# Fillers in the waits for the norms, VectorE alone for the merge sum, small matmuls padded to 128 rows

## What is computed

```
hn    = rmsnorm(h) ;  u = hn @ w_in              # q, k, v, gates of four mixers, and 4 x 1024 merge logits
y_sb, y_gla, y_ml, y_ret = four causal mixers of u, each 256 wide
merged = sum over n of sigmoid(logits_n + b_n) * (y_n @ w_branch_n)
h     = h + rmsnorm(merged @ w_out)
f     = rmsnorm(h)
h     = h + rmsnorm((silu(f @ w_gate) * (f @ w_up)) @ w_down)
```

## Time and profile before

| | |
|---|---|
| median of 3 runs | 1014.35 us (1011.94 to 1016.44) |
| profiled execution | 1014.39 us, its span 1012.6 us |
| TensorE busy | 982.7 us (97%), 7664 matmuls |
| VectorE, ScalarE, GpSimd busy | 592.2, 520.7, 128.1 us |
| mean granted clock | 0.991 |

### The profile page before, as it was taken

How to read it: one execution, slowest core, us unless ns; L and a number is a source line. 1 busy time by engine, 2 the same in 40 slices (tenths; PEclk the granted TensorE clock), 3 DMA queues, 4 the chain that set the end, 5 groups by cost and what they waited for, 6 DMA issues and landing times.

```text
span 1012.6 us, 19561 instructions
## 1 busy us (share of the span) xinstructions
PE 982.7 (97%) x7664; PEld 931.5 (92%) x7664; DVE 592.2 (58%) x870; ACT 520.7 (51%) x826; POOL 128.1 (13%) x106
## 2 busy tenths in 40 slices
PE   7999999999998999999989999999999899999997
PEld 5999888789997999999969998888999899999996
DVE  6556565346966655553465565744579656666443
ACT  4553754366466544454455437544754755454452
POOL 1000000002540222110000000000034212222010
PEclk9999999999999999999989999999999999999998
DMA  5874434246552655555545544344465536555551
GB/s 157 271 229 130 128 120 126 84 125 160 174 169 82 206 167 166 170 191 162 163 125 164 169 139 125 112 126 126 125 162 172 167 125 187 186 183 190 188 187 42
DMA packets 168523, 156.42 MB, mean 154 GB/s; under 512 B 9091, under 2 KB 167022, under 8 KB 168078
## 3 DMA queue, kind: packets, MB, share of 16 engines
q1 hardware_dynamic: 167598, 152.13, 48.7%
q10 hardware_dynamic: 672, 3.37, 1.0%
q0 software_dynamic: 192, 0.07, 0.0%
HBM read 154.50 MB, written 1.05 MB: 154 GB/s over the span
## 4 chain that ended last, share of the span: by engine, by line
PE 92%; DVE 4%; ACT 2%; issue 1%; DMA 1%; SPq 0%; DVEq 0%; ACTq 0%
PE banks L622 26%; PE banks L624 25%; PE banks L623 25%; PE banks L672 2%; PE banks L657 1%; PE banks L653 1%; PE banks L654 1%; PE banks L868 1%; DVE lo L1377 1%; PE banks L870 1%; ACT hi L1039 1%; PE banks L897 1%; PE banks L905 1%; DVE term L1648 1%; DMA xt<-in_x 1%
## 5 line engine op out<-in xcount | busy, mean ns | idle before, releaser
L622 PE MATMUL banks<-xh,hi 128*128 128x272 f32 (+1 forms) x1584 | 460.1, 290 | 2.4 <-DVE lo L1377 1.3
L1377 DVE TENSOR_TENSOR lo<-raw,hi 128x1024 fp32r<-128x1024 f32 (+1 forms) x290 | 356.4, 1232 | 174.8 <-ACT hi L1039 173.6
L624 PE MATMUL banks<-xh,lo 128*128 128x272 f32 (+1 forms) x1584 | 452.9, 286 | 0.0
L623 PE MATMUL banks<-xl,hi 128*128 128x272 f32 (+1 forms) x1584 | 452.8, 286 | 0.0
L1039 ACT ACTIVATE hi<-raw 128x1024 fp32r<-128x1024 f32 (+1 forms) x290 | 302.0, 1042 | 96.5 <-PE banks L624 58.0
L622 PEld LDWEIGHTS banks<-xh,hi 128*128 128x128 f32 x1584 | 298.5, 188 | 9.5 <-issue 6.6
L623 PEld LDWEIGHTS banks<-xl,hi 128*128 128x128 f32 x1584 | 298.0, 188 | 0.6
L624 PEld LDWEIGHTS banks<-xh,lo 128*128 128x128 f32 x1584 | 298.5, 188 | 0.0
L624 PE MATMUL banks<-ah,lo 128*128 128x272 f32 (+1 forms) x352 | 100.4, 285 | 0.0
L622 PE MATMUL banks<-ah,hi 128*128 128x272 f32 (+1 forms) x352 | 100.1, 284 | 0.0
L623 PE MATMUL banks<-al,hi 128*128 128x272 f32 (+1 forms) x352 | 99.9, 284 | 0.0
(11 more groups left out here) (252 smaller groups left out, 1176.4 us busy)
## 6 DMA issues: line engine op xcount, KB each, us to landing
raw<-in_w_in SPq DMA_DIRECT2D x54, 1024.0 KB, 5.2
raw<-in_ffn_w_gate SPq DMA_DIRECT2D x22, 1024.0 KB, 5.3
raw<-in_ffn_w_up SPq DMA_DIRECT2D x22, 1024.0 KB, 5.3
raw<-in_ffn_w_down SPq DMA_DIRECT2D x16, 1024.0 KB, 5.1
raw<-in_w_out SPq DMA_DIRECT2D x8, 1024.0 KB, 5.2
raw<-in_w_in SPq DMA_DIRECT2D x12, 512.0 KB, 4.4
raw<-in_w_branch SPq DMA_DIRECT2D x12, 512.0 KB, 5.6
raw<-in_ffn_w_down SPq DMA_DIRECT2D x8, 768.0 KB, 4.3
```

The source lines that it names most:

```text
L622: mm(dst, wh, mh, start=start, stop=False)
L623: mm(dst, wh, ml, start=False, stop=False)
L624: return mm(dst, wl, mh, start=False, stop=stop)
L1377: tt(lo[g % 2][:, 0:k, f], raw[g % 2][:, 0:k, f], hi[g % 2][:, 0:k, f].bitcast(F32), ALU.subtract).then_inc(lo_ready, 2 if g in G_MIX else 1)
```

## The change

- Fillers: eight instead of four at the start; four after `mean_square_first`, three after the mean square of layer 1's first norm, and four after the mean square of norms 1 and 3 in both layers.
- Sums of squares at the start by half rows of x, each as soon as its half has come; the first mean square is then five matmuls instead of three.
- Roundings: `round_half(0)` and its `lo` go ahead of the first root; in `gate_up` one half is rounded ahead of `root(l, 2)`, and its `lo` goes between the two gate tiles on VectorE. `add_sublayer` adds tile 0 before it scales tile 1.
- Merge: GpSimd's `merge` is gone; VectorE does both additions for every m, right behind the two products. `rest_of_merged(m)` is now in round m itself for m = 0 to 5, behind `rest_of_half`; for m = 6 and 7 in round 7. ScalarE's order is as it was.
- Padding to 128 rows: `wgate`, `gl` and `gr_rows` get 128 partitions; the meta tokens' values of heads 2 and 3 get tiles of their own (`v0b`, `v0c`), zero elsewhere, so that L868 multiplies with all rows of `pt0`. This adds memsets on VectorE (`wgate`, `v0b`, and `v0c` behind the last step of `conv`); the DMA of `wgate` on GpSimd's queue waits for its memset, and the two bias DMAs behind it too.

Not shown in the diff: the tiles' new places, two semaphores that fall away, `turn` writing through `meta_values` and waiting for five pads, and the memset of `v0b`.

```
@@ -227,7 +227,7 @@
 REST_AHEAD = 3
-WARM_START = 4
+WARM_START, WARM_FIRST, WARM_NORM, WARM_PRE = 8, 4, 4, 3
@@ -333,12 +333,12 @@
 ifbias = sb("ifbias", [P, DEPTH])
-wgate = sb("wgate", [16, DEPTH, P])
+wgate = sb("wgate", [P, DEPTH, P])
...
 ones = sb("ones", [P, T])
-gl = sb("gl", [36, T])
-gr_rows = sb("gr_rows", [36, HEADS, T])
+gl = sb("gl", [P, T])
+gr_rows = sb("gr_rows", [P, HEADS, T])
@@ -411,6 +410,12 @@
+
+def meta_values(mix, pair):
+
+    if pair == 0:
+        return M["v0"][:, mix, :]
+    return M["v0b" if mix in (SB, RET) else "v0c"][:, mix // 3 if mix in (SB, RET) else mix - GLA, :]
@@ -689,9 +694,11 @@
         ps = open_tile(t)
-        pe.wait_ge(ss_ready, 6)
-        for b, (at, n) in enumerate(((0, META), (KB1, P), (KB2, P))):
-            last = mm(ps[:, at:at + n], cut["mean"][0:n, :], sq[0:n, b, 0:n], start=True, stop=True)
+        pe.wait_ge(ss_ready, 10)
+        mm(ps[:, 0:META], cut["mean"][0:META, :], sq[0:META, 0, 0:META], start=True, stop=True)
+        for b, at in enumerate((KB1, KB2)):
+            for n in range(2):
+                last = mm(ps[:, at:at + P], cut["mean"], sq[:, 1 + 2 * b + n, 0:P], start=n == 0, stop=n == 1)
@@ -731,7 +738,7 @@
         pe.wait_ge(bias_loaded, 48)
-        close_tile(mm(open_tile(t)[:, 0:T], wgate[:, l, :], M["small"][0:16, :], start=True, stop=True), t)
+        close_tile(mm(open_tile(t)[:, 0:T], wgate[:, l, :], M["small"][:], start=True, stop=True), t)
@@ -864,8 +871,7 @@
             wait_p(l, mix, h)
-        both = head_rows[pair % 2]
-        mm(ops[:, 0:T], M["v0"][both, mix, :], M["pt0"][both, :], start=True, stop=False)
+        mm(ops[:, 0:T], meta_values(mix, pair), M["pt0"][:], start=True, stop=False)
@@ -992,14 +998,19 @@
             mean_square(l, 0, 0)
+            keep_warm(WARM_PRE)
...
             mean_square_first()
+            keep_warm(WARM_FIRST)
...
         mean_square(l, 1, q_start(l))
+        keep_warm(WARM_NORM)
...
         mean_square(l, 3, q_start(l))
+        wait_taken(pe, TILE[l]["gu"] + 2)
+        keep_warm(WARM_NORM)
@@ -1050,17 +1061,18 @@
-        ss, spare = sq[:, KT - 1, 0:3], (sub[:, 0:4, 0:256], sub[:, 4:8, 0:256])
+        ss, spare = sq[:, KT - 1, 0:5], sub[:].rearrange("p k t -> p (k t)")
         act.wait_ge(meta_loaded, 16)
-        fn(spare[0][0:META], xt[0:META, 0, :].rearrange("p (a c) -> p a c", a=4), ACT.Square, accum_out=ss[0:META, 0:1]).then_inc(ss_ready, 1)
-        act.wait_ge(x_loaded[0], 16)
-        act.wait_ge(x_loaded[1], 16)
-        for b in range(1, 3):
-            act.wait_ge(ss_ready, b)
-            fn(spare[b % 2], xt[:, b, :].rearrange("p (a c) -> p a c", a=4), ACT.Square, accum_out=ss[:, b:b + 1]).then_inc(ss_ready, 1)
-        for b, n in enumerate((META, P, P)):
-            act.wait_ge(ss_ready, 3)
-            fn(sq[0:n, b, 0:n], cut["ident"][0:n, 0:n], ACT.Copy, scale=ss[0:n, b:b + 1]).then_inc(ss_ready, 1)
+        fn(spare[0:META, 0:D], xt[0:META, 0, :], ACT.Square, accum_out=ss[0:META, 0:1]).then_inc(ss_ready, 1)
+        for n in range(2):
+            act.wait_ge(x_loaded[n], 16)
+            for b in range(1, 3):
+                at = 2 * b - 1 + n
+                act.wait_ge(ss_ready, 1)
+                fn(spare[:, 512 * (at - 1):512 * at], xt[:, b, 512 * n:512 * n + 512], ACT.Square, accum_out=ss[:, at:at + 1]).then_inc(ss_ready, 1)
+        for at, n in enumerate((META, P, P, P, P)):
+            act.wait_ge(ss_ready, 5)
+            fn(sq[0:n, at, 0:n], cut["ident"][0:n, 0:n], ACT.Copy, scale=ss[0:n, at:at + 1]).then_inc(ss_ready, 1)
@@ -1301,7 +1313,8 @@
         for c in range(2):
-            round_half(n + c)
+            if c:
+                round_half(n + 1)
@@ -1333,8 +1346,8 @@
             square_first()
+            round_half(0)
             root(l, 0, 0)
-            round_half(0)
@@ -1348,6 +1361,7 @@
         round_ffn_x(l, q0)
+        round_half(2 * G_GU[l] + ROUND_AHEAD)
@@ -1381,12 +1395,12 @@
+        if l == 0:
+            rest_of_half(0)
...
                 stt(sq[:, k, :], hT[:, k, :], par[:, l, R_MIXPRE + k:R_MIXPRE + k + 1], rstd[:], ALU.mult, ALU.mult).then_inc(xn_ready[l], 1)
-            if l == 0 and k == 1:
-                rest_of_half(0)
@@ -1400,12 +1414,19 @@
+
+        def scale(k):
+            tt(sub[:, k, q0:], sub[:, k, q0:], rstd[:, q0:], ALU.mult).then_inc(post_scaled[l], 1)
+
+        scale(0)
         for k in range(KT + 2):
+            if 0 < k < KT - 1:
+                scale(k + 1)
             if k < KT:
-                tt(sub[:, k, q0:], sub[:, k, q0:], rstd[:, q0:], ALU.mult).then_inc(post_scaled[l], 1)
-            if 0 < k <= KT:
-                dve.wait_ge(post_scaled[l], n // 2 * KT + k)
-                tt(hT[:, k - 1, q0:], hT[:, k - 1, q0:], sub[:, k - 1, q0:], ALU.add).then_inc(h_ready[l], 1)
+                dve.wait_ge(post_scaled[l], n // 2 * KT + k + 1)
+                tt(hT[:, k, q0:], hT[:, k, q0:], sub[:, k, q0:], ALU.add).then_inc(h_ready[l], 1)
+            if k == 0:
+                scale(1)
@@ -1477,6 +1499,9 @@
                 stt(M["mqk"][:, t, :], src, tap, M["mqk"][:, t, :], ALU.mult, ALU.add).then_inc(conv_step[l], 1)
+        if j == 3:
+            dve.wait_ge(conv_step[l], 16)
+            nc.vector.memset(M["v0c"][:], 0.0).then_inc(pad_set[l], 1)
@@ -1642,25 +1667,24 @@
             dve.wait_ge(merge_step[l], m - 1)
+        t = term[:, m % 2, :, q0:]
...
             n = slice(2 * pair, 2 * pair + 2)
-            tt(term[:, m % 2, n, q0:], branch_banks[(2 * m + pair) % 3][:, :, 0:T - q0], by_branch[:, n, m, q0:], ALU.mult).then_inc(branch_free[l], 1)
+            tt(t[:, n, :], branch_banks[(2 * m + pair) % 3][:, :, 0:T - q0], by_branch[:, n, m, q0:], ALU.mult).then_inc(branch_free[l], 1)
         if m == KT - 1:
-            last = term[:, m % 2, :, q0:]
-            dve.wait_ge(branch_free[l], 2 * KT)
-            tt(last[:, 0:2, :], last[:, 0:2, :], last[:, 2:4, :], ALU.add).then_inc(half_late[l], 1)
-            rest_of_merged(l, m - 2)
-            dve.wait_ge(half_late[l], 1)
-            dve.wait_ge(ml_ready[l], KT - 2)
-            tt(acc[:, m % 2, q0:], last[:, 0, :], last[:, 1, :], ALU.add).then_inc(half_late[l], 1)
-        else:
-            rest_of_half(at + REST_AHEAD)
-        if m and m != KT - 2:
             rest_of_merged(l, m - 1)
+        dve.wait_ge(branch_free[l], 2 * m + 2)
+        tt(t[:, 0:2, :], t[:, 0:2, :], t[:, 2:4, :], ALU.add).then_inc(half_ready[l], 1)
+        dve.wait_ge(half_ready[l], m + 1)
+        if m >= 2:
+            dve.wait_ge(ml_ready[l], m - 1)
+        tt(acc[:, m % 2, q0:], t[:, 0, :], t[:, 1, :], ALU.add).then_inc(merge_step[l], 1)
...
             rest_of_merged(l, m)
-            rest_of_half(at + REST_AHEAD)
+        rest_of_half(at + REST_AHEAD)
+        if m < KT - 2:
+            rest_of_merged(l, m)
@@ -1692,10 +1716,9 @@
-        for c in range(2):
-            gate_tile(c, t + c)
-            if c:
-                rest_of_half(n + 1)
+        gate_tile(0, t)
+        rest_of_half(n + 1)
+        gate_tile(1, t + 1)
@@ -1716,10 +1739,11 @@
     nc.vector.memset(ones[:], 1.0).then_inc(misc_set, 1)
+    nc.vector.memset(wgate[:], 0.0).then_inc(misc_set, 1)
...
     nc.vector.memset(gr_rows[:], 0.0).then_inc(misc_set, 1)
-    dve.wait_ge(misc_set, 5)
+    dve.wait_ge(misc_set, 6)
@@ -1770,27 +1794,13 @@
-    def merge(l):
-
-        q0 = q_start(l)
-        for m in range(KT - 1):
-            pool.wait_ge(branch_free[l], 2 * m + 2)
-            if m:
-                pool.wait_ge(merge_step[l], m)
-            tt(half[:, :, q0:], term[:, m % 2, 0:2, q0:], term[:, m % 2, 2:4, q0:], ALU.add).then_inc(half_ready[l], 1)
-            pool.wait_ge(half_ready[l], m + 1)
-            if m >= 2:
-                pool.wait_ge(ml_ready[l], m - 1)
-            tt(acc[:, m % 2, q0:], half[:, 0, q0:], half[:, 1, q0:], ALU.add).then_inc(merge_step[l], 1)
...
     load_rows(pool, PARAM_ROWS[7:], par_late)
-    pool.dma_start(wgate[:], gla_w_gate_up.rearrange("l r m -> r l m")).then_inc(bias_loaded, 16)
-    pool.wait_ge(misc_set, 1)
+    pool.wait_ge(misc_set, 3)
+    pool.dma_start(wgate[0:16], gla_w_gate_up.rearrange("l r m -> r l m")).then_inc(bias_loaded, 16)
...
         q0 = q_start(l)
-        merge(l)
```

More of the change, by code:

```diff
@@ L378, in build @@
                     ("conv_in", [P, 4, T + 3]), ("mqk", [P, 4, T]), ("gq", [P, T]), ("gk", [P, T]),
-                    ("gr", [P, 2, T]), ("mo", [P, 2, T]), ("rg", [P, 2, T]), ("v", [P, 2, 4, 256]), ("v0", [P, 4, P]),
+                    ("gr", [P, 2, T]), ("mo", [P, 2, T]), ("rg", [P, 2, T]), ("v", [P, 2, 4, 256]), ("v0", [P, 4, P]), ("v0b", [P, 2, P]),
                     ("pt", [P, HEADS, SCW]), ("pt0", [P, T]), ("sa", [P, 2, SCW]), ("sb2", [P, 2, SCW]),
@@ L382, in build @@
                     ("rows", [P, 3, T]), ("osb", [P, 8, T])]
-        gla_spec = [("qa", [P, SEQ]), ("qb", [P, P]), ("q0", [P, META]), ("kr0", [P, KB2]), ("kr1", [P, SEQ]), ("k00", [P, 32])]
```

(15 more changed lines are left out.)

## The result

The changed kernel takes 1023.64 us (median of 4 runs, 1022.43 to 1025.22), the kernel before 1014.28 in the same job: a ratio of 1.0094, 95% interval 1.0066 to 1.0121. It is slower by 9.4 us; predicted were 1015.5 us and a range of 1006 to 1021. The profiled execution took 1025.22 us, its span is 1023.4 against 1012.6.

What follows compares the result with a forecast made beforehand. TensorE, busy 97% of the span, was taken to bound the kernel. Gains of 15.3 us against 16.6 lost in the merge: 1014.4 - 15.3 + 16.6 = 1015.7, stated as 1015.5, range 1006 to 1021 (0.8).

Steps and rivals of the forecast that it cites:

- the ring: Merge: `lo`, transfer, `hi`, rounding of the merged tile, its rest, next `lo`: 7.5 to 8.3 us a round against TensorE's 6.07.
- Merge: Both layers' merges: 7.2 us lost in layer 0, 8.4 in layer 1, 1 for the clock of both: 16.6 (12 to 19).
- Adding tile 0 first brings the first add one scaling earlier: `add_sublayer`: 0.25 us gained at each of the three borders that TensorE waits at, 0.7 in all.
- Together 4.2: Fillers: 1.0 us back from the matmuls from 518.15, 3.2 from two half-clock stretches; between 1 and 4.5.
- Padding: Full rows in the small matmuls of both layers gain 5.1 us, between 3 and 6.
- The small matmul over 16 rows: Once per layer: full rows save 0.39 us, from 1.10 to 0.71, 0.8 for both.
- The values: L868: the matmul behind it follows after 0.65 us where 0.45 would do; 0.2 each, 16 times: 3.1.
- The exponents that stand alone: Pair over 36 rows: 0.4 us saved where alone, twice per layer, 1.6; among the scores -0.2 per layer.
- The rival by which padding exposes loads: 42 padded matmuls each start late by some 0.2 us, 8.4 in all, and 5.1 is not gained: 1029.2; chance 0.04.
- Gate and up: TensorE's wait of 1.10 us in layer 0 and a little longer one in layer 1 go: 2.3 us gained.
- Start: +0.2 us from the clock before the root, 1.2 from the `lo`, 1.6 from `first`: 3.0 gained, between 0 and 4.5.
- the merge is free: Rival: the merge costs nothing, VectorE having 5.1 us of work in a round of 6.07: 997.7; chance 0.15.

Runs made afterwards that it cites:

- experiment 1: Changed kernel with round m again taking the rest of merged tile m - 1, additions still on VectorE: 1006.45 us, ratio 0.9897 to the kernel before.
- experiment 3: Kernel before with only the rest of merged tile m moved into round m, GpSimd's sums kept: 1034.89 us, ratio 1.0187.
- experiment 10: Changed kernel with the rest of merged tile m in its own round but behind the odd half's `lo`: 1007.03 us, ratio 0.9926 to the kernel before.
- experiment 8: Experiment 7's kernel without the fillers at the norm borders, those at the start kept: 1006.71 us, ratio 0.9911 to the kernel before.
- experiment 4: Experiment 1's kernel with the old order of scalings and adds (scaling k before add k - 1): 1002.27 us, ratio 0.9875 to the kernel before.
- experiment 7: Experiment 1's kernel, tile 0 still added first, each rest (`xl`) taken one step earlier: 1002.73 us, ratio 0.9884 to the kernel before.
- experiment 12: Experiment 7's kernel with the two `lo` in VectorE's first norm behind rests 3 and 5 instead of 1 and 4: 1002.23 us, ratio 0.987.
- experiment 9: Experiment 7's kernel with four fillers at the start and none behind the first mean square, border fillers kept: 1004.26 us, ratio 0.9895.

## Why the prediction was wrong

It had the ring, its place and its sign, and said that the two big sums were of one size. It foretold +1.3 us on the trace, measured are +10.8. Of these 9.5 us the borders make 4.9, the merge 3.1 and padding 1.9; start and gate/up nearly cancel. By its own steps:

**Merge: the mechanism right, one term too small.** Predicted were 15.6 us of waits and 1 for the clock. Of the 19.7 in the table, steps of a quarter microsecond or more (waits less the one of the earlier trace rows at 283.03 that went) make 7.6 and 7.4, 15.0 together; 48 matmuls behind them, 0.21 to 0.23 us apart instead of some 0.12 to 0.13, make 2.0 and 2.6. So half clock costs 4.6, not 1: that term had no row under it, though the kernel before shows at the earlier trace rows what a wait of this length can bring, 1.6 us each time. The round of the ring is 9.9 and then 8.65 us, not 7.5 to 8.3: in the first the 1 MB transfer took 6.8 us, where I took the 4.4 and 5.2 of the earlier trace rows. The sum of the waits came out right all the same; that TensorE's head start took up the first long round is argued, not shown. Experiments 1, 3 and 10 show the cause: the moved wait alone, and only through what stands behind it.

**Borders: the step that failed.** "Adding tile 0 first brings the first add one scaling earlier ... 0.7" had the wrong sign. I followed the first `xh` and not the next thing TensorE wants from VectorE, the first `xl`, which went two operations back. That is a wait of 1.04 and of 0.97 us in the two norms 1, and in layer 0 half clock behind it (some 1.4). With it fell a part of "Together 4.2": both steps together were to give 4.9 and in the table give 0.0 (+2.5, -1.9, -0.6). Taken by itself each part of the fillers' term was near: with the order mended they give 2.7 to 4.0 at the borders (experiment 8), where I had 4.2. The row at 518.15 that I named for a wait between a mean square and the first tile is the wait ahead of layer 1's first mean square; the waits before first tiles are 2.86 and 2.78 us (shown at the end), so the sum does not change. The order alone costs 1.3 us (by ratio) to 4 (by medians); in the traces of experiments 4 and 7 it is 2.3 to 2.4 in each layer, half clock included.

**Padding: 5.1 predicted, 3.2 in the table.** Three of its terms fell short. The small matmul over 16 rows saves nothing: padded, it does enter 0.12 us behind its neighbour as foretold, but the way out is as long as before. TensorE's timeline of the changed kernel:

```profile
35.07 0.29 PE L629 MATMUL banks<-xh,lo 128*128 128x272 f32 x1
35.19 0.62 PE L741 MATMUL banks<-small,wgate 128*128 128x272 f32 x2
35.94 0.36 PE L627 MATMUL banks<-xh,hi 128*128 128x272 f32 x1
36.14 0.28 PE L628 MATMUL banks<-xl,hi 128*128 128x272 f32 x1
```

From 35.07 to 36.14 are 1.07 us, against 1.10 in the earlier trace rows and the 0.71 that I took from the earlier trace rows. A price taken from another matmul, inside a dense stretch, was carried over to this one; why its exit is dearer is not shown. That is 0.8 less. The values give the 0.2 that I had (0.19: the entry is 0.13 instead of 0.22, the next start 0.55 behind instead of 0.65) at 14 of the 16 places. At the two others (the second pair of the first mixer, in each layer) TensorE waits for ScalarE's `osb`, and gives back the 0.2 of the pair before: again some 0.8 less. The exponents that stand alone give 0.37 each where I had 0.4; where they stand among the scores full rows cost 0.34 a layer and not 0.2. The rival by which padding exposes loads is out: behind a fast matmul the padded ones start 0.12 to 0.13 later. The Trainium skill, TensorE: Matmul & The Clock Gate, Part 3, says that a load overlaps matmuls in flight only if its row group differs; that is not what these rows show. The same part also says that a load into the background weight buffer is pulled ahead of matmuls in flight; that would fit these rows, but no run here shows which buffer a load goes to.

**Gate and up: right,** 2.9 for 2.3; no wait stands at the fifth tile in either layer. **Start: near,** 2.4 for 3.0: transposes come in groups of 0.53 us (0.83 before), 1.0 us later; the first `xh` matmul is 3.0 earlier, and a wait of 1.2 us for an `xl` behind a `lo` takes back a part. Experiment 12 moves it and gains nothing. How near is partly luck, as the starts of equal kernels differ by 2 us (experiment 9).

Of the rivals, "the merge is free" (997.7) is what experiments 1, 4 and 7 come nearest to, at 1002.3 to 1006.5. None was "ring and more half clock", though the upper edge should have held it: 16.6 could be 19 by late transfers, and the borders' terms (4.9) could be nothing, which is 1023 together. I took the edges one at a time.

## What to carry to other kernels

Before a wait is moved in an in-order queue, list what stands behind it there, follow each to the transfer or buffer that it frees, and see whether that comes back to the thing waited for; if it does, the length of that circle against the bound engine's round is the price, and one place further back may cost nothing. When a sequence of an engine is reordered, ask of every product, not of the first, which operations now stand ahead of it. A wait of TensorE costs itself and can cost again by the clock behind it (2.99 and 3.73 us did here, 2.95 did not), so price it both ways. Fillers ahead of a further wait may not hold the clock.

## What the runs showed of the hardware

The granted clock of the windows does not show the slow stretch at the start. In experiment 9 the windows say 1.00 from 0 on, yet the first matmuls are 0.22 us apart, as they are in stretches shown at 0.50:

```profile
16.00:18.00 2.00, 1.06 (x5) 1.09 (x5) 1.86 (x5) 1.63 (x3) 0.00 (x0) 1.00 1.01 348
```

```profile
17.53 0.43 PE L662 MATMUL banks<-xl,hi 128*128 128x272 f32 x1
17.76 0.43 PE L658 MATMUL banks<-xh,hi 128*128 128x272 f32 x1
17.99 0.43 PE L659 MATMUL banks<-xh,lo 128*128 128x272 f32 x1
```

Starts of neighbouring matmuls tell the level more surely than the column, and a mean granted clock leaves the start out.

Waits of one length can be followed by either level. In the kernel before, TensorE's timeline at the norm 1 of layer 0 and of layer 1, and the windows there:

```profile
309.29 0.36 PE L653 MATMUL banks<-xh,hi 128*128 128x272 f32 x1 [2.86 <-ACT xh L1085]
...
806.09 0.45 PE L653 MATMUL banks<-xh,hi 128*128 128x256 f32 x1 [2.78 <-ACT xh L1085]
```

```profile
309.00:312.00 3.00, 2.71 (x17) 2.42 (x17) 3.00 (x9) 2.48 (x8) 0.00 (x0) 1.00 0.00 0
...
806.00:809.00 3.00, 2.91 (x11) 2.71 (x12) 3.00 (x10) 2.53 (x7) 0.00 (x0) 0.53 0.02 5
```

So one trace with half clock, or without it, does not settle what brought it.
